# Attention outputs kept by features and divided there by sums that go through memory, in place of two transposes

## The chip, the cores and the metric

The kernel runs as one program on one core of a Trainium2 chip. The time is the device time of one execution in microseconds (us). The kernel before takes 1885.41 us (median of 3 runs, 1884.92 to 1886.67).

The engines have these names in the profile: PE is TensorE (matrix products), PEld its loads of stationary operands, DVE is VectorE, ACT is ScalarE, POOL is GpSimd, SP is SyncE, which here only issues transfers.

## The reference

One encoder layer on x of 1024 tokens by 1024 features, in float32:

```python
h = rms_norm(x, ffn1_norm_g);  x = x + 0.5 * swiglu_ffn(h, ffn1...)
h = rms_norm(x, mix_norm_g);   proj = h @ w_in            # 1024 x 3584
aq, ak, av, hq, hf, hi, hg = jnp.split(proj, 7 x 512)
# A: 8 heads x 64, queries of a 64-token chunk see their own chunk and the 8 before
scores = q_chunk @ k_band.T * 64**-0.5 + bias;  p = softmax(scores);  attn_out = p @ v_band
# B: 4 heads x 128, gated linear recurrence, then a norm and a gate -> hgrn_out
x = x + concat([attn_out, hgrn_out], -1) @ w_out          # 1024x1024 @ 1024x1024
h = rms_norm(x, ffn2_norm_g);  x = x + 0.5 * swiglu_ffn(h, ffn2...)
```

The change touches only what lies between `p @ v_band` and the product with `w_out`.

## The kernel before

The program is written out by hand, engine by engine, with semaphores between them; each engine works its list off in order. A float32 product is made of three faster ones: each operand is split into a high part (`...hi`, written by ACT) and the remainder (`...lo`, written by DVE), and PE multiplies hi by hi, hi by lo and lo by hi (lines 710 to 712). So the left operand of the output projection has to be there as `hThi` and `hTlo`: eight tiles `k` of 128 features, each 128 partitions (features) by 1024 tokens. Tiles 0 to 3 are attention's features (a pair of heads each), 4 to 7 the recurrence's.

Attention goes over four pairs of heads. A pair has 12 units of at most 128x640 scores (two per step, one for each head), so there are 48 units `v` in 24 steps `w`; pair p has the steps 6p to 6p+5. In step w PE issues, in this order: the scores of units 2w and 2w+1 (line 1031); the transposes of the exponentials of unit 2w-2 (`turn`, 1044); the products with v of the two units before (`values(w-2)`, 1064); the transposes of unit 2w-1. Between them `halves` puts transposes of the next pair's q and k (1089), and those of attention's outputs (`turn_out`, 1099). DVE does for each unit `maxima` (bias added, row minimum of the negative, 2123), for two units of three the copy of the transposed exponentials out of PSUM (2134; ACT does the third, 1532), and in steps 1 to 4 of a pair the sums of squares and the normalisation of the next pair's q and k (2087, 2094). ACT makes the exponentials, with their row sums in `psumr` (1549). Scores of step w+1 are written into the banks that `maxima` has read, so PE waits for `unit_max` there.

`values` gives outputs with the features on the partitions and the tokens along the row, not yet divided by the sums of the exponentials. Those sums lie the other way: a token on each partition. So the kernel before does this: ACT copies the output to `outT` (1524); PE turns four 128x128 tiles into bank 7 (`turn_out`, eight times four in all); DVE inverts the sums and multiplies while it copies into `cat` (tokens on the partitions; `head_output`, 2105 and 2109). For the projection, PE turns all of `cat` back, eight transposes per tile of 128 tokens (`turn_cat`, 766, for the first two, `turn_tile`, 751, for the other six), ACT copies the 128x1024 result from PSUM into `hThi` (1222), DVE subtracts into `hTlo` (1654). The recurrence's outputs come into `cat` by a transfer and need this one transpose in any case.

The output projection has 16 rows `d` (8 tiles of tokens times two halves of the output), each of 24 products 128x512. Between the first rows PE issues the transposes of the tile two rows ahead, and after row 0 the last `turn_out`. SP's list around here: q, k, bias and v of the pairs 2 and 3, then the stores of x for the second feed-forward.

Of the kernel before, what the change touches and what calls it, by code (L numbers as in the profile page):

```python
# [24 lines left out]
P = 128  # L25
T = 1024
# [147 lines left out]


OUT_STEPS = NU // 2
# [4 lines left out]


def out_step(p, g):
    return OUT_STEPS * (p + 1) + (0 if g == 0 else 1 if p == PAIRS - 1 else 2)

# [11 lines left out]
def turn_bank(R, t):  # L197

    if R == R_FFN1:
        return (2, 6)[t % 2]  # L200
    if R == R_FFN2:
        return (2, 0, 2, 0, 2, 0, 2, 6)[t]
    if R == R_MIX:
        return (4, 6, 4, 6, 0, 2, 0, 2)[t]
    return 2 * (t % 2)
# [19 lines left out]
def build(nc, x, ffn1_norm_g, ffn1_w_gate, ffn1_w_up, ffn1_w_down, mix_norm_g, w_in, attn_q_norm_g,  # L225
# [3 lines left out]
    with ExitStack() as ctx:  # L229
# [7 lines left out]
        wd_d = nc.dram_tensor("wd_scratch", [4, NPAIR, P, HALF], F32, kind="Internal").ap()  # L237
        x_d = nc.dram_tensor("x_scratch", [T, D], F32, kind="Internal").ap()
# [54 lines left out]
        with ExitStack() as c:  # L293
# [11 lines left out]
            rcp = keep("rcp", [P, 2, 2, TT], where=c)  # L305
            outT = keep("outT", [P, 2, T], where=c)
# [15 lines left out]
        with ExitStack() as c:  # L322
            cat = keep("cat", [P, TT, D], where=c, side="right")
# [107 lines left out]
        lb_diff = sem("lb_diff")  # L431
        lb_sig = sem("lb_sig")
        lb_ready = sem("lb_ready")
# [47 lines left out]
        out_turned = sem("out_turned")  # L481
        rcp_ready = sem("rcp_ready")
        head_out = sem("head_out")
# [22 lines left out]
        def _(sp):  # L506
# [161 lines left out]

            out_pieces(0)
# [36 lines left out]
        def _(pe):  # L706
# [19 lines left out]
            def turn_tile(R, t):  # L726

                r = TT * R + t
                if R == R_CAT:
                    src = cat[:, CAT_ORDER[t], :]  # L730
                    pe.wait_ge(hT_ready, r - 1)
                else:
                    pe.wait_ge(y_ready, TT * norm_no(R) + t + 1)
                    src = y_slot(R, t)
# [20 lines left out]
            def turn_cat(t, h):  # L755


                if h and t == 0:
                    pe.wait_ge(cat_loaded, 16)
                    pe.wait_ge(unit_max, NV)  # L760
                elif h == 0 and t == 0:
                    pe.wait_ge(head_out, 2 * PAIRS - 1)
                c0 = turn_bank(R_CAT, t) * HALF + h * HALF
                for k in range(4):
                    at = h * HALF + k * P
                    mm = pe.transpose(ps[:, c0 + k * P:c0 + (k + 1) * P], cat[:, CAT_ORDER[t], at:at + P], ident[:, :])
                if h == 0:
                    mm.then_inc(turned, 1)
# [300 lines left out]
            def wait_half_bank(what, p, n):  # L1069

                if what == "qk":
                    if n:
                        pe.wait_ge(qkT_ready, 4 * p + n)
                    elif p > 1:
                        pe.wait_ge(head_out, 2 * (p - 2) + 2)
                elif n == 0:
                    if p < PAIRS - 1:
                        pe.wait_ge(qkT_ready, 4 * p + 8)
                    else:
                        pe.wait_ge(head_out, 2 * (p - 1) + 2)  # L1080
                else:
                    pe.wait_ge(head_out, 2 * p + 1)

            def turn_half(p, n):

                pe.wait_ge(qk_normed, 2 * p + n // 2 + 1)
                wait_half_bank("qk", p, n)
# [5 lines left out]
            def turn_out(p, g):  # L1093
                pe.wait_ge(outT_ready, NU * p + (NU - 4 if g == 0 else NU))
                wait_half_bank("out", p, g)
                for t in range(4):
                    c0 = (4 * (1 - g) + t) * P
                    b = 7 * HALF
                    mm = pe.transpose(ps[:, b + t * P:b + (t + 1) * P],
                                      outT[:, p % 2, c0:c0 + P], ident[:, :])  # L1100
                mm.then_inc(out_turned, 1)

            def halves(w, place):
                p, step = w // OUT_STEPS, w % OUT_STEPS
                if place == 0:
                    for g in range(2):
                        for q in range(PAIRS - 1 if g else PAIRS):
                            if out_step(q, g) == w:
                                turn_out(q, g)
# [10 lines left out]
            for w in range(STEPS + 2):  # L1120
# [6 lines left out]
                if w == STEPS:  # L1127
                    turn_cat(0, 1)
                    turn_cat(1, 1)
# [3 lines left out]
                if w == STEPS + 1:  # L1133
                    turn_cat(0, 0)
# [5 lines left out]
            turn_cat(1, 0)  # L1140


            for h in range(2):
                for t in range(TT):
# [3 lines left out]
                    if h == 0 and t == 2:  # L1148
                        pe.wait_ge(head_out, 2 * PAIRS)
# [21 lines left out]
                    if d == 0:  # L1171
                        turn_out(PAIRS - 1, 1)
                    if h == 0 and t + 2 < TT:
                        turn_tile(R_CAT, t + 2)
# [10 lines left out]
        def _(act):  # L1185
# [25 lines left out]
            def hT_hi(R, t):  # L1211
# [3 lines left out]
                if R == R_CAT:  # L1215
                    if t == 0:
                        act.wait_ge(unit_out, NV)
                    t = CAT_ORDER[t]
                elif R == R_MIX:
                    t = MIX_ORDER[t]  # L1220
                src = ps[:, c0:c0 + D].rearrange("p (k c) -> p k c", k=KT)
                act.activation(hThi[:, :, t * P:(t + 1) * P], src, ACT.Copy).then_inc(hT_hi_ready, 1)

# [275 lines left out]
            act.wait_ge(lb_diff, 1)  # L1499
# [926 lines left out]
```

## Time and profile before

| | |
|---|---|
| runs | 1884.92, 1885.41, 1886.67 us |
| profiled execution | 1885.16 us, of which the span from the first to the last instruction is 1883.6 us |
| PE busy | 1869.4 us, 9171 products and transposes |
| DVE, ACT, POOL busy | 1125.0, 675.3, 406.7 us |
| granted TensorE clock | 1.00 over the whole span |
| attention | about 1030 to 1145 us of the span |
| output projection with transposes of `cat` | 1145 to about 1190 us |

Busy time of PE counts each matmul from its start to its modelled end, and these overlap: what one costs is read from the distance between two starts, not from its own duration. "Idle before" in brackets is the time for which the engine stood still ahead of an instruction, and behind it who released it.

### The profile page before, as it was taken

How to read it: one execution, taken by the hardware profiler on the slowest of the kernel's cores; microseconds unless marked ns; L12 is line 12 of the kernel's file. 1: busy time of each engine (PE TensorE's matmuls, PEld its weight loads, DVE VectorE, ACT ScalarE, POOL GpSimd, SP SyncE). 2: the span in 40 equal slices, each digit the busy share in tenths (PEclk: the TensorE clock that was granted, in tenths of full speed). 3: DMA queues.
4: the chain of work that ended last, by engine and by line, in shares of the span. 5: the costliest groups of instructions: out<-in, count | busy, mean ns of one | idle time of the engine just before them, and what ended most of it. 6: DMA issues, size and time to landing. Idle time of an engine off the chain costs nothing. (4 is left out here: it accounts for less than half of the span.)

```text
span 1883.6 us, 24459 instructions
## 1 busy us (share of the span) xinstructions
PE 1869.4 (99%) x9171; PEld 1546.3 (82%) x9171; DVE 1125.0 (60%) x1591; ACT 675.3 (36%) x1029; POOL 406.7 (22%) x319
## 2 busy tenths in 40 slices
PE   9999999999999999999999999999999999999999
PEld 8888888888888888888888678888888888888887
DVE  6966665665546641156667874477666656655464
ACT  7422323333333533211223663353223233333332
POOL 2043422241103110002222310000434222411030
PEclk9999999999999999999999999999999999999999
DMA  5355444436866433434433510133554444368653
GB/s 182 112 196 190 146 162 168 153 138 244 318 195 197 131 122 124 138 101 140 134 132 106 162 60 1 68 112 112 196 190 146 163 167 153 138 244 306 219 192 140
DMA packets 221341, 296.52 MB, mean 157 GB/s; under 512 B 15377, under 2 KB 117913, under 8 KB 221234
## 3 DMA queue, kind: packets, MB, share of 16 engines
q1 hardware_dynamic: 206752, 262.19, 41.0%
q0 software_dynamic: 6272, 18.14, 3.0%
q10 hardware_dynamic: 8210, 14.75, 2.0%
q8 instruction: 68, 1.11, 0.2%
q14 instruction: 39, 0.32, 0.1%
HBM read 206.13 MB, written 92.56 MB: 159 GB/s over the span
## 5 line engine op out<-in xcount | busy, mean ns | idle before, releaser
L710 PE MATMUL ps<-hThi,whi 128*128 128x512 f32 x888 | 346.6, 390 | 0.2 <-DVE hid L1751 0.2
L712 PE MATMUL ps<-hThi,wlo 128*128 128x512 f32 x888 | 345.5, 389 | 0.0
L711 PE MATMUL ps<-hTlo,whi 128*128 128x512 f32 x888 | 345.5, 389 | 0.0
L710 PE MATMUL ps<-whi 128*128 128x512 f32 x616 | 240.0, 390 | 0.0
L712 PE MATMUL ps<-whi,wlo 128*128 128x512 f32 x616 | 239.7, 389 | 0.0
L711 PE MATMUL ps<-wlo,whi 128*128 128x512 f32 x616 | 239.6, 389 | 0.0
L710 PEld LDWEIGHTS ps<-hThi,whi 128*128 128x128 f32 x888 | 166.7, 188 | 34.9 <-issue 0.9
L712 PEld LDWEIGHTS ps<-hThi,wlo 128*128 128x128 f32 x888 | 166.7, 188 | 34.7
L711 PEld LDWEIGHTS ps<-hTlo,whi 128*128 128x128 f32 x888 | 166.7, 188 | 34.3
L710 PE MATMUL ps<-hXhi,whi 128*128 128x512 f32 x480 | 186.9, 389 | 0.8 <-issue 0.8
L712 PE MATMUL ps<-hXhi,wlo 128*128 128x512 f32 x480 | 186.8, 389 | 0.0
L711 PE MATMUL ps<-hXlo,whi 128*128 128x512 f32 x480 | 186.7, 389 | 0.0
L1723 DVE TENSOR_TENSOR wlo<-raw,whi 128x512 fp32r<-128x512 f32 x176 | 127.3, 727 | 98.1 <-ACT whi L1280 98.1
L710 PE MATMUL ps<-whi,hThi 128*128 128x512 f32 x440 | 176.5, 401 | 0.0
L712 PE MATMUL ps<-whi,hTlo 128*128 128x512 f32 x440 | 171.7, 390 | 0.0
L711 PE MATMUL ps<-wlo,hThi 128*128 128x512 f32 x440 | 171.6, 390 | 0.0
L1835 DVE TENSOR_TENSOR wlo<-raw,whi 128x1024 fp32r<-128x1024 f32 x80 | 107.5, 1343 | 80.5 <-ACT whi L1332 80.3
L1280 ACT ACTIVATE whi<-raw 128x512 fp32r<-128x512 f32 x176 | 109.7, 627 | 120.6 <-PE ps L712 120.6
L1835 DVE TENSOR_TENSOR wlo<-rawx,whi 128x1024 fp32r<-128x1024 f32 x74 | 95.2, 1286 | 87.2 <-ACT whi L1332 87.2
L710 PEld LDWEIGHTS ps<-whi 128*128 128x128 f32 x616 | 115.6, 188 | 24.1
L712 PEld LDWEIGHTS ps<-whi,wlo 128*128 128x128 f32 x616 | 115.6, 188 | 23.9
L711 PEld LDWEIGHTS ps<-wlo,whi 128*128 128x128 f32 x616 | 115.6, 188 | 23.8
(220 smaller groups left out, 2828.7 us busy)
## 6 DMA issues: line engine op xcount, KB each, us to landing
hid_scratch<-hid SPq DMA_DIRECT2D x132, 256.0 KB, 3.3
raw<-ffn_w_gate SPq DMA_DIRECT2D x44, 512.0 KB, 3.8
raw<-ffn_w_up SPq DMA_DIRECT2D x44, 512.0 KB, 4.9
wdb<-ffn_w_down SPq DMA_DIRECT2D x44, 512.0 KB, 4.1
wd_scratch<-wdb SPq DMA_DIRECT2D x88, 256.0 KB, 4.3
raw<-hid_scratch SPq DMA_DIRECT2D x80, 256.0 KB, 2.8
rawx<-hid_scratch SPq DMA_DIRECT2D x74, 256.0 KB, 2.8
raw<-w_in SPq DMA_DIRECT2D x28, 512.0 KB, 5.4
```

The lines of the kernel that those rows point to most:

```text
L710: pe.matmul(dst, ahi, bhi, start=first, stop=False, skip_group_check=onto)
L711: pe.matmul(dst, ahi, blo, start=False, stop=False, skip_group_check=onto)
L712: return pe.matmul(dst, alo, bhi, start=False, stop=last, skip_group_check=onto)
L1280: act.activation(weight(whi, w, F), raw_weight(w), ACT.Copy).then_inc(w_hi_ready, 1)
L1723: dve.tensor_tensor(weight(wlo, w, F), raw_weight(w), weight(whi, w, F).bitcast(F32), ALU.subtract).then_inc(w_ready, 1)
L1835: dve.tensor_tensor(wlo[:, s, :], raw_piece(n), whi[:, s, :].bitcast(F32), ALU.subtract)\
```

## The change

- ACT copies attention's outputs to `catT`, which holds all four pairs by features (128 x 4 x 1024). `turn_out` and the multiplication out of bank 7 are gone, and with them the waits of q's and k's transposes for that bank.
- DVE inverts the sums of a pair at once (`invert_sums`, at unit 2 of the next pair; for the last pair in two halves, at units 45 and 48). SP stores the inverses to memory (`store_rcp`), tokens in order, and loads them back as rows, each repeated on the 64 partitions of its head (`load_rcp`, to `rowr`). DVE multiplies `catT` by `rowr` in place, 128x512 at a time (`norm_out`, at units 9 and 11 of the next pair; for the last pair behind the loop and behind `add(1)`).
- Only the recurrence's half (`cath`) is turned for the projection, four transposes per tile of tokens into one bank of four, four tiles ahead (`turn_cat`). ACT and DVE write `hThi` and `hTlo` in two instructions each, one from PSUM and one from `catT` (`cat_hi`, `cat_lo`).
- Three semaphores of the lower bound `lb` become one.

```diff
-def out_step(p, g):
-    return OUT_STEPS * (p + 1) + (0 if g == 0 else 1 if p == PAIRS - 1 else 2)
+def cat_bank(t):
+    return t % 4
...
+        rcp_d = nc.dram_tensor("rcp_scratch", [PAIRS, TT, 2, P], F32, kind="Internal").ap()
...
-            rcp = keep("rcp", [P, 2, 2, TT], where=c)
-            outT = keep("outT", [P, 2, T], where=c)
+            rcp = keep("rcp", [P, 2, TT, 2], where=c)
+            rowr = keep("rowr", [P, 2, T], where=c)
...
-            cat = keep("cat", [P, TT, D], where=c, side="right")
+            catT = keep("catT", [P, PAIRS, T], where=c, side="right")
+            cath = keep("cath", [P, TT, HALF], where=c, side="right")
...
+            def store_rcp(p, g=None):
+                tiles = slice(0, TT) if g is None else slice(4 * (1 - g), 4 * (1 - g) + 4)
+                sp.wait_ge(rcp_ready, p + 1 + (g or 0))
+                sp.dma_start(rcp_d[p, tiles].rearrange("t h p -> p (t h)"),
+                             rcp[:, p % 2, tiles, :].rearrange("p t h -> p (t h)"),
+                             allow_slow_non_contiguous=True).then_inc(rcp_stored, 16)
+            def load_rcp(p, g=None):
+                tiles = slice(0, TT) if g is None else slice(4 * (1 - g), 4 * (1 - g) + 4)
+                sp.wait_ge(rcp_stored, 16 * (p + 1 + (g or 0)))
+                if p >= 2:
+                    sp.wait_ge(out_normed, 2 * (p - 2) + 2)
+                for hd in range(2):
+                    row = rcp_d[p, tiles, hd:hd + 1, :].rearrange("t h p -> h t p")
+                    sp.dma_start(rowr[hd * DH:(hd + 1) * DH, p % 2, tiles.start * P:tiles.stop * P]
+                                 .rearrange("r (t p) -> r t p", p=P),
+                                 row.to_broadcast([DH, tiles.stop - tiles.start, P])).then_inc(row_loaded, 16)
...
                 load_qk(p)
+                store_rcp(p - 2)
                 sp.wait_ge(unit_out, NU * (p - 1))
                 load_bias(p)
                 load_v(p)
+                load_rcp(p - 2)
+            store_rcp(PAIRS - 2)
+            load_rcp(PAIRS - 2)
+            for g in range(2):
+                store_rcp(PAIRS - 1, g)
+                load_rcp(PAIRS - 1, g)
...
-            def turn_out(p, g):
-                pe.wait_ge(outT_ready, NU * p + (NU - 4 if g == 0 else NU))
-                wait_half_bank("out", p, g)
-                for t in range(4):
...
-                if p >= 2 and 2 * w % NU == 0:
-                    act.wait_ge(out_turned, 2 * (p - 2) + 2)
...
-                    last = act.activation(outT[:, p % 2, t * P:(t + 1) * P], ps[:, b:b + P], ACT.Copy)
+                    last = act.activation(catT[:, p, t * P:(t + 1) * P], ps[:, b:b + P], ACT.Copy)
...
+            def cat_hi(t):
+                act.wait_ge(turned, TT * R_CAT + t + 1)
+                if t == 0:
+                    act.wait_ge(unit_out, NV)
+                at = slice(CAT_ORDER[t] * P, (CAT_ORDER[t] + 1) * P)
+                act.activation(hThi[:, 4:KT, at], bank(cat_bank(t)).rearrange("p (k c) -> p k c", k=4), ACT.Copy)
+                act.wait_ge(out_normed, 2 * PAIRS - (1 if t < 4 else 0))
+                act.activation(hThi[:, 0:4, at], catT[:, :, at], ACT.Copy).then_inc(hT_hi_ready, 1)
...
-            def head_output(p, g):
...
+            def norm_out(p, g):
+                cols = slice(HALF * (1 - g), HALF * (1 - g) + HALF)
+                dve.wait_ge(row_loaded, 32 * (p + 1 + (g if p == PAIRS - 1 else 0)))
+                dve.wait_ge(outT_ready, NU * p + (NU - 4 if p == PAIRS - 1 and g == 0 else NU))
+                dve.tensor_tensor(catT[:, p, cols], catT[:, p, cols], rowr[:, p % 2, cols], ALU.mult)\
+                   .then_inc(out_normed, 1)
...
+                if v == NV - 3:
+                    invert_sums(PAIRS - 1, 0)
+                if v >= NU and v < NV:
+                    p = v // NU - 1
+                    if v % NU == 2:
+                        invert_sums(p)
+                    if v % NU in (9, 11):
+                        norm_out(p, (v % NU - 9) // 2)
+                if v == NV:
+                    invert_sums(PAIRS - 1, 1)
+            norm_out(PAIRS - 1, 0)
+            cat_lo(0)
+            cat_lo(1)
```

How the instructions stand now. First DVE at step 6 (units 12 and 13, the first of pair 1): `ISA S,nmax` is one unit's `maxima`, `COPY PT` the copy of transposed exponentials. Before:

```order
L2134 COPY PT<-ps 128x640 [waits unit_out,unit_turned]
L2105 RECIPROCAL rcp<-psumr 128x2x4 [waits unit_exp,ro_stored]
L2109 TENSOR_TENSOR cat<-ps,rcp 128x4x128 [waits out_turned,rcp_ready]
L2123 ISA S,nmax<-ps,bias 128x640 [waits unit_exp,unit_scores]
L2123 ISA nmax 128x1
L2123 ISA S,nmax<-ps,bias 128x640 [waits unit_exp,unit_scores]
```

and now:

```order
L2137 COPY PT<-ps 128x640 [waits unit_out,unit_turned]
L2126 ISA S,nmax<-ps,bias 128x640 [waits unit_exp,unit_scores]
L2126 ISA nmax 128x1
L2126 ISA S,nmax<-ps,bias 128x640 [waits unit_exp,unit_scores]
L2126 ISA nmax 128x1
L2137 COPY PT<-ps 128x640 [waits unit_out,unit_turned]
L2105 RECIPROCAL rcp<-psumr 128x2x8 [waits unit_exp]
L2126 ISA S,nmax<-ps,bias 128x640 [waits unit_exp,unit_scores]
```

The reciprocal and the multiplication no longer stand between the two maxima of step 6; a reciprocal of twice the width stands between those of step 7. Next PE from the last `turn_out` of the attention loop to the projection's first product. Before:

```order
L1099 MATMUL ps<-ident,outT 128x128 [waits head_out,outT_ready]
L1099 MATMUL ps<-ident,outT 128x128 x3
L1064 MATMUL ps<-PT,v_in 64x128 [waits outT_ready,PT_by_vector,PT_by_scalar]
L1064 MATMUL ps<-PT,v_in 64x128 x9
L1044 MATMUL ps<-ident,Pr 128x128 [waits PT_by_vector,unit_exp]
L1044 MATMUL ps<-ident,Pr 128x128 x4
L766 MATMUL ps<-ident,cat 128x128 [waits head_out]
L766 MATMUL ps<-ident,cat 128x128 x3
L1064 MATMUL ps<-PT,v_in 64x128 [waits outT_ready,PT_by_scalar,PT_by_vector]
L1064 MATMUL ps<-PT,v_in 64x128 x9
L766 MATMUL ps<-ident,cat 128x128 x4
L720 MATMUL ps<-whi,hThi 128x512 [waits split_lo,hT_hi_ready]
```

and now:

```order
L1084 MATMUL ps<-PT,v_in 64x128 [waits outT_ready,PT_by_vector,PT_by_scalar]
L1084 MATMUL ps<-PT,v_in 64x128 x9
L1064 MATMUL ps<-ident,Pr 128x128 [waits PT_by_vector,unit_exp]
L1064 MATMUL ps<-ident,Pr 128x128 x4
L786 MATMUL ps<-ident,cath 128x128 x4
L1084 MATMUL ps<-PT,v_in 64x128 [waits outT_ready,PT_by_scalar,PT_by_vector]
L1084 MATMUL ps<-PT,v_in 64x128 x9
L786 MATMUL ps<-ident,cath 128x128 x4
L747 MATMUL ps<-whi,hThi 128x512 [waits split_lo,hT_hi_ready]
```

The four transposes of `outT` are gone there, and the transposes of the recurrence's half need nothing of DVE. Last DVE from the copy of unit 45 to the projection's first subtractions, now:

```order
L2137 COPY PT<-ps 128x640 [waits unit_out,unit_turned]
L2113 TENSOR_TENSOR catT<-catT,rowr 128x512 [waits outT_ready,row_loaded]
L2137 COPY PT<-ps 128x640 [waits unit_out,unit_turned]
L2105 RECIPROCAL rcp<-psumr 128x2x4 [waits unit_exp]
L2113 TENSOR_TENSOR catT<-catT,rowr 128x512 [waits outT_ready,row_loaded]
L1651 TENSOR_TENSOR hTlo<-ps,hThi 128x4x128 [waits hT_hi_ready]
L1653 TENSOR_TENSOR hTlo<-catT,hThi 128x4x128
L1651 TENSOR_TENSOR hTlo<-ps,hThi 128x4x128 [waits hT_hi_ready]
L1653 TENSOR_TENSOR hTlo<-catT,hThi 128x4x128
```

Before, the projection's first subtraction followed upon the last copy, one reciprocal and one multiplication; now a multiplication that waits for a transfer (`row_loaded`) stands ahead of it.

## Rows read from the trace of the kernel before

**Rows 1.** The page, busy time of each engine.

```profile
PE 1869.4 (99%) x9171; PEld 1546.3 (82%) x9171; DVE 1125.0 (60%) x1591; ACT 675.3 (36%) x1029; POOL 406.7 (22%) x319
```

**Rows 2.** PE's waits over the span: total us, times, longest.

```profile
PE ps L1031 <- DVE nmax L2123: 3.0, 6, 0.8
```

**Rows 3.** Transposes of cat and outT: ns min/median/max, first and last start.

```profile
L751 PE MATMUL ps<-ident,cat x48: 270/272/273, 1151.1 to 1183.6; 128*128 128x128 f32 x48
...
L766 PE MATMUL ps<-ident,cat x16: 272/273/328, 1137.4 to 1144.2; 128*128 128x128 f32 x16
...
L1099 PE MATMUL ps<-ident,outT x32: 270/272/273, 1058.3 to 1151.0; 128*128 128x128 f32 x32
```

**Rows 4.** PE's timeline, steps 6 to 9: start, us, what, idle before.

```profile
1056.45 1.35 PE L1031 MATMUL ps<-kT,qT 64*128 64x512 f32 x8
...
1061.02 1.35 PE L1031 MATMUL ps<-kT,qT 64*128 64x512 f32 x8 [0.15 <-DVE nmax L2123]
...
1064.94 1.35 PE L1031 MATMUL ps<-kT,qT 64*128 64x512 f32 x8
...
1069.37 1.35 PE L1031 MATMUL ps<-kT,qT 64*128 64x512 f32 x8
```

**Rows 5.** DVE's timeline, steps 6 to 12 and step 22.

```profile
1059.31 0.19 DVE L2105 RECIPROCAL rcp<-psumr 128x8 f32<-128x8 f32 x1
1059.54 0.69 DVE L2109 TENSOR_TENSOR cat<-ps,rcp 128x512 f32<-128x512 f32 x1
...
1060.89 0.08 DVE L2123 DVE_READ_ACCUMULATOR2_ANT nmax<- 128x1 f32 x1
...
1063.89 0.81 DVE L2123 CUSTOM_DVE_ANT_0 S<-ps,bias 128x640 f32<-128x640 f32 x1
...
1080.00 0.82 DVE L2134 COPY PT<-ps 128x640 f32<-128x640 f32 x1
...
1081.72 0.56 DVE L2123 CUSTOM_DVE_ANT_0 S<-ps,bias 128x384 f32<-128x384 f32 x1 [0.90 <-PE ps L1031]
...
1084.80 0.82 DVE L2134 COPY PT<-ps 128x640 f32<-128x640 f32 x1 [1.34 <-PE ps L1044]
...
1086.07 0.82 DVE L2123 CUSTOM_DVE_ANT_0 S<-ps,bias 128x640 f32<-128x640 f32 x1 [0.45 <-PE ps L1031]
...
1133.72 0.82 DVE L2134 COPY PT<-ps 128x640 f32<-128x640 f32 x1 [0.18 <-PE ps L1044]
```

**Rows 6.** PE's timeline around row 1 of the projection.

```profile
1150.67 0.60 PE L1099 MATMUL ps<-ident,outT 128*128 128x128 f32 x4
1151.11 1.04 PE L751 MATMUL ps<-ident,cat 128*128 128x128 f32 x8
...
1157.48 1.03 PE L751 MATMUL ps<-ident,cat 128*128 128x128 f32 x8
```

**Rows 7.** Timeline at the projection's start, ACT and PE.

```profile
1143.98 1.02 ACT L1222 ACTIVATE hThi<-ps 128x1024 fp32r<-128x1024 f32 x1 [1.51 <-PE ps L1064]
...
1145.06 0.50 PE L720 MATMUL ps<-whi,hThi 128*128 128x512 f32 x1 [0.59 <-ACT hThi L1222]
```

**Rows 8.** ACT's copies of half that width, from the first feed-forward.

```profile
L1227 ACT ACTIVATE hThi<-ps x8: 578/593/623, 11.1 to 23.8; 128x512 fp32r<-128x512 f32 x8
```

**Rows 9.** DMA issues: KB each, median us from issue to landing.

```profile
raw<-ffn_w_gate SPq DMA_DIRECT2D x44, 512.0 KB, 3.8
...
raw<-hid_scratch SPq DMA_DIRECT2D x80, 256.0 KB, 2.8
...
tok_scratch<-y ACTq DMA_DIRECT2D x40, 256.0 KB, 2.0
...
v_in<-tok_scratch SPq DMA_DIRECT2D x4, 512.0 KB, 5.4
...
bias_scratch<-tot POOLq DMA_DIRECT2D x2, 128.0 KB, 5.5
...
lbs<-hgrn_lower_bounds POOLq DMA_DIRECT2D x1, 4.0 KB, 4.8
```

More of the change, by code:

```diff
@@ L728, in turn_tile @@
                 r = TT * R + t
[L729 to L734, printed above, removed]
+                pe.wait_ge(y_ready, TT * norm_no(R) + t + 1)
+                src = y_slot(R, t)
                 if R == R_MIX:
@@ L1091, in turn_half @@
                 mm.then_inc(qk_turned, 1)
-            def turn_out(p, g):
-                pe.wait_ge(outT_ready, NU * p + (NU - 4 if g == 0 else NU))
-                wait_half_bank("out", p, g)
-                for t in range(4):
[L1097 to L1101, printed above, removed]
-            def halves(w, place):
[L1104 to L1109, printed above, removed]
+            def halves(w, place):
+                p, step = w // (NU // 2), w % (NU // 2)
                 if p + 1 < PAIRS:
@@ L1139, in _ @@
                 halves(w, 1)
-            turn_cat(1, 0)
+            turn_cat(3)
             for h in range(2):
@@ L1170, in _ @@
                     mm.then_inc(row_done, 1)
[L1171 to L1174, printed above, removed]
+                    if h == 0 and t + 4 < TT:
+                        turn_cat(t + 4)
                     if h == 1 and t >= 1:
@@ L1498, in _ @@
             group(0, 0, ACT.Silu, True)
-            act.wait_ge(lb_diff, 1)
-            act.activation(lb[:, 0, :], lb[:, 2, :], ACT.Sigmoid).then_inc(lb_sig, 1)
-            act.wait_ge(lb_ready, 1)
+            act.wait_ge(lb_step, 1)
+            act.activation(lb[:, 0, :], lb[:, 2, :], ACT.Sigmoid).then_inc(lb_step, 1)
+            act.wait_ge(lb_step, 3)
             group(1, 0, ACT.Sigmoid, True)
@@ L1557, in _ @@
                 if v == NV + 2:
-                    hT_hi(R_CAT, 0)
+                    cat_hi(0)
                 if v >= 4 and v % 2 == 0:
@@ L1564, in _ @@
             for t in range(1, TT):
-                hT_hi(R_CAT, t)
+                cat_hi(t)
             for q in range(4):
@@ L1655, in hT_lo, with cat_lo @@
                                   hThi[:, k0:KT, t * P:(t + 1) * P].bitcast(F32), ALU.subtract)\
+                   .then_inc(hT_ready, 1)
+            def cat_lo(t):
+                dve.wait_ge(hT_hi_ready, TT * R_CAT + t + 1)
+                at = slice(CAT_ORDER[t] * P, (CAT_ORDER[t] + 1) * P)
+                dve.tensor_tensor(hTlo[:, 4:KT, at], bank(cat_bank(t)).rearrange("p (k c) -> p k c", k=4),
+                                  hThi[:, 4:KT, at].bitcast(F32), ALU.subtract)
+                dve.tensor_tensor(hTlo[:, 0:4, at], catT[:, :, at], hThi[:, 0:4, at].bitcast(F32), ALU.subtract)\
                    .then_inc(hT_ready, 1)
@@ L2098, in _, with invert_sums @@
                           lambda: norm_qk(0, 1)])
-            def head_output(p, g):
-                tiles = slice(4 * (1 - g), 4 * (1 - g) + 4)
-                dve.wait_ge(unit_exp, NU * p + (NU if g else NU - 4))
-                dve.reciprocal(rcp[:, p % 2, :, tiles], psumr[:, p % 2, :, tiles]).then_inc(rcp_ready, 1)
-                dve.wait_ge(rcp_ready, 2 * p + g + 1)
-                dve.wait_ge(out_turned, 2 * p + g + 1)
-                r = rcp[:, p % 2, :, tiles].rearrange("p h t -> p t h").unsqueeze(3).to_broadcast([P, 4, 2, DH])
-                dve.tensor_tensor(cat[:, tiles, p * P:(p + 1) * P].rearrange("p t (h d) -> p t h d", d=DH),
-                                  bank(7).rearrange("p (t h d) -> p t h d", t=4, d=DH), r, ALU.mult)\
-                   .then_inc(head_out, 1)
+            def invert_sums(p, g=None):
+                tiles = slice(0, TT) if g is None else slice(4 * (1 - g), 4 * (1 - g) + 4)
+                dve.wait_ge(unit_exp, NU * p + (NU - 4 if g == 0 else NU))
+                if p >= 2 and not g:
+                    dve.wait_ge(rcp_stored, 16 * (p - 1))
+                dve.reciprocal(rcp[:, p % 2, tiles, :].rearrange("p t h -> p h t"), psumr[:, p % 2, :, tiles])\
+                   .then_inc(rcp_ready, 1)
+            def norm_out(p, g):
[4 more added lines that the diff above has]
+                   .then_inc(out_normed, 1)
             dve.wait_ge(proj_done, PROJ_OUTS)
@@ L2169, in _ @@
                 add(t, CAT_ORDER[t], 0)
+                if t == 1:
+                    norm_out(PAIRS - 1, 1)
                 if t + 2 < TT:
-                    hT_lo(R_CAT, t + 2)
+                    cat_lo(t + 2)
             for t in range(TT):
```

80 lines of the change are left out of this document (24 added, 56 removed).

## The prediction

> **What bounds the kernel now.** I read the page's busy times first: PE is busy for 1869.4 us of 1883.6 [rows 1], so what PE does is paid almost everywhere. PE's waits come next, to see where the few idle microseconds lie: 3.0 us in six places before scores, for DVE's row maxima, the longest 0.8 [rows 2], and 0.59 us before the first product of the output projection, for ACT's copy to `hThi` [rows 7]. Both lie inside the stretch that the change touches, so there PE's work alone doesn't decide: each place needs a look at whether DVE or ACT ends close behind PE. For that I read the timelines of PE and DVE over attention's steps, then the start of the projection. The reader is to see three things in them: the pitch of the steps, how late DVE's last maximum is against PE's next scores, and which instruction comes just before the first product of the projection.
>
> **What PE loses.** 96 transposes concern `outT` and `cat`: 48, 16 and 32 [rows 3]. Of them 32 (`outT`) go and 32 of the 64 of `cat` go. Their own 272 ns is not their price, since they overlap: four cost 1151.11 - 1150.67 = 0.44 us when they stand in a row with others [rows 6], 0.11 each. So:
>
> - Projection, 32 transposes of `cat`: 32 x 0.11 = 3.5 us. A row with eight of them lasts 1157.48 - 1151.11 = 6.37 us [rows 6]; ACT's copy takes 1.02 of that [rows 7], and two of half the width 1.2 [rows 8], so the split copies are hidden behind PE there, and DVE's, which are some 0.2 longer as well.
> - The last `turn_out`, behind row 0: 0.44 us.
> - The `turn_out` of the last pair in step 24: 0.44 to 0.53, I take 0.5; the steps' own rows say the same as follows.
>
> **Attention's steps.** Step 6 lasts from 1056.45 to 1061.02, 4.57 us; step 7, without `turn_out`, 3.92; step 8, with one, 4.43 [rows 4]. So step 6 has 0.65 too much and step 8 0.51 too much. In step 6 four transposes (0.44) don't explain all of it: PE's next scores waited 0.15 us for DVE [rows 4], whose last maximum ended at 1060.97 [rows 5], because the multiplication into `cat` (0.69 us, at 1059.54) stood between the two maxima. The change takes both away, the transposes from PE and the multiplication from DVE's place between the maxima. Without them DVE's last maximum would end some 0.9 earlier, and PE's 3.92 decides. The pattern comes three times (pairs 1 to 3): 3 x (0.65 + 0.51) = 3.5 us. The third pair gives nearly the same, so I don't correct for it.
>
> What comes in instead:
> - The reciprocal of a pair, now in steps 7, 13, 19 between the maxima. Bounds: nothing, or its whole 0.19 (for half the width) [rows 5]. In step 7 DVE's last maximum starts at 1063.89 and ends about 0.8 later, at 1064.7, PE's scores start at 1064.94 [rows 4, 5]: the cover is about 0.2 before a semaphore's way. I take 0.1 each, 0.3 in all.
> - `norm_out` at unit 9 of a pair, behind the copy that starts at 1080.00 and ends at 1080.82: DVE is then idle for 0.90 until 1081.72 [rows 5], and a 128x512 multiplication takes 0.69 from PSUM (its row), from SBUF I take 0.73. Hidden. At unit 11 it stands behind the copy that starts at 1084.80; the next maximum started at 1086.07 after 0.45 idle, so it is 0.2 to 0.3 late. That step is a former step 6 or 12 with its 0.2 of slack: I take 0.1 in all, between 0 and 0.6.
> - ACT's copies to `catT` are those to `outT`, and waits for bank 7 only go.
>
> **The start of the projection.** The first product waits for ACT's copy, which starts at 1143.98 and takes 1.02 [rows 7]. Now it is two copies of half the width, 0.59 each [rows 8], which overlap by some 0.05 to 0.1: 0.1 to 0.2 more, I take 0.15. The second of them waits for `norm_out` of the last pair, and that for the row of inverse sums: a store and two loads behind the reciprocal at unit 45. This is the only new wait on PE's path with no great cover, and it holds all that is behind it: `cat_hi` on ACT with the last `keep_out`, `cat_lo` on DVE, and the projection's first product on PE.
>
> Its cover: the reciprocal follows the copy of 1133.72, so it ends near 1134.7 [rows 5]. The second copy of ACT would start at 1143.98 + 0.5 less the 0.5 us of the gone `turn_out`, about 1144.0, and `norm_out` takes 0.73 and some 0.1 to be seen. So store plus loads have about 8.5 us. For pair 2 the time from the reciprocal (unit 38, near 1120.7) to its use (unit 45, 1134.5, less 0.4 of step 20) is about 13.5 us; for pairs 0 and 1, from 1064.1 to 1080.7 less 0.5, about 16 us.
>
> Its price: no row shows a store of 4-byte pieces. The store of the last pair's half has 1024 of them, of a whole pair 2048. From below: a store of 128 rows, 2.0 us. From above: 512 pieces of 256 bytes to memory took 5.5 (`bias_scratch<-tot`); less 2.0 that is 6.8 ns a piece, so 9.0 for 1024 and 16 for 2048. Nearest in kind is the load of 1024 values of 4 bytes, `lbs`, 4.8 us on POOL's queue; I take it, and 2.0 + 2 x 2.8 = 7.6 for 2048. The loads have pieces of 512 bytes: two of 128 KB together like one of 256 KB, 2.8, with the second issue 3.0; of a whole pair 1024 pieces and 512 KB, 3.8 as `raw<-ffn_w_gate`, at worst 5.4 as `v_in` [rows 9]. So the last half needs 4.8 + 3.0 + 0.2 for semaphores = 8.0 of 8.5, pair 2 needs 7.6 + 3.8 + 0.2 = 11.6 of 13.5, the first two pairs 11.6 of 16, where bias and v loads stand between on SP's list, but are issued at once. All hidden, with 0.5 us to spare at the tightest place. I take 0 for it, with -0 to +4 as its range there.
>
> The Trainium skill, page "DMA: Bandwidth & Descriptors", speaks against this store in two places: its overview gives 512 bytes as the least piece for full rate, with read-modify-write below, and its list of patterns (the row on a strided last dimension) says that such a transfer becomes one descriptor per element. The row of `lbs` bears the second out at most weakly (4 KB took 4.8 us, 256 KB took 2.0), and no row shows the first at 4 bytes. By the page's measured table (10.5 ns for each packet on one of 16 engines, 2 us fixed) the store would take an estimated 2.7 us and not come near its cover. What a slow store would do is the first rival.
>
> **Sum.** -3.5 (cat transposes) -0.44 (last turn_out) -0.5 (turn_out of step 24) -3.5 (steps 6, 8 and their like) +0.3 (reciprocals) +0.1 (norm_out) +0.15 (two copies) = -7.4 us. From the profiled execution's 1885.16: 1877.8. The median of the runs is 0.25 above the profiled one, so 1878.1 us.
>
> **The rivals.**
> - *The row comes late (slower at the far end).* Let e be what 1024 pieces cost beyond 2.0 us (I took 2.8). The last half starts to hold PE at e = 8.5 - 2.0 - 3.2 = 3.3, pair 2 at (13.5 - 6.0)/2 = 3.75, pairs 0 and 1 at (16 - 6.0)/2 = 5. DVE's wait for a row stops maxima and copies, and PE within one step. Mild case, e = 5: about 2.5 at pair 2 and 1 or 2 at the end, total 1878.1 + 4 = 1882. Bad case, e = 7 (the corner stores' rate): 6.5 + 2 x 4, with the end covered by the stop at pair 2, which lets the last store go out while DVE stands: +14.5, total 1892.6. Slower than before by 0.2% needs e above 6.4. For it: one row at that rate per piece. Against: those pieces were 64 times as large, and on POOL's queue, whose 4-byte load took less for twice the pieces [rows 9].
> - *DVE sets the pace of the steps.* If in the steps with 3.92 us DVE's round (scores, maximum, copy, maximum) is the real bound, and the gains of steps 6 and 8 were only DVE's, nothing is lost; but if the new reciprocal and norm_out cost their full time, 3 x 0.2 + 3 x 0.7, the gain there is 0.8 instead of 3.1: 1880.4. For it: the ends in rows 4 and 5 are within 0.2 us of each other. Against: norm_out stands where rows show 0.90 and 0.45 of idle time.
> - *The stretch gives nothing in attention:* another wait (ACT's exponentials) keeps the steps at 4.5; then only 4.2 are left: 1881.2. Against: step 7 has the same ACT work and runs at 3.92.
>
> **How the numbers follow.** Forecast 1878.1, chance 0.70; row late, mild 0.12 (1880 to 1884), bad 0.04; DVE's pace 0.08; nothing in attention 0.04; the remaining 0.02 for a gain above 8.2, if PE's wait at the projection shrinks as well. A measurement of this kernel can tell about 0.2%, 3.8 us, from no change: faster is below 1881.6. The forecast, DVE's pace, half of the mild case and most of the fourth are faster: 0.86, which I lower to 0.83 for what I don't see; same 0.12; slower 0.05. The range 1877.0 to 1882.5 holds the forecast with its unknown costs (1877.2 to 1879), both pace cases and half of the mild one.
>
> **What the profile of the changed kernel would show.** PE with 9107 instructions (64 fewer); steps 6, 8, 12, 14, 18, 20 at 3.9 to 4.0 us between scores, as step 7; rows of the projection at 5.9 us, and 5.5 for the last ones, in place of 6.3; DVE's idle time before `norm_out` on a DMA near zero for pairs 0 to 2; `rcp_scratch<-rcp` landing in 3 to 8 us; the first product's wait for ACT still about 0.6 to 0.8 us. The forecast is wrong if PE waits more than 1 us there, if DVE waits for `rowr`, or if scores wait for maxima in steps 7 and 12 by more than 0.3.

## The result and the profile after

The changed kernel takes 1896.44 us (median of 4 runs, 1894.51 to 1898.25) against 1885.18 before (median of 4 runs): ratio 1.0058, interval 1.0046 to 1.0070. It is slower by 0.6%, where 1878.1 us, faster by 0.4%, was forecast. Its profiled execution took 1894.51 us, with a span of 1892.3.

The page of the changed kernel, busy time of each engine, answers to [rows 1]:

```profile
PE 1864.7 (99%) x9107; PEld 1541.7 (81%) x9107; DVE 1123.0 (59%) x1596; ACT 676.2 (36%) x1037; POOL 407.9 (22%) x319
```

PE has its 64 instructions fewer. Its waits, total us, times, longest, answer to [rows 2]:

```profile
PE ps L747 <- ACT hThi L1216: 9.5, 1, 9.5
PE ps L1051 <- DVE nmax L2126: 2.5, 3, 0.8
PE ps L1064 <- ACT PT L1524: 2.5, 2, 1.3
...
PE ps L786 <- DVE nmax L2126: 1.4, 1, 1.4
```

Scores wait for maxima three times, no longer six. But the projection's first product waits 9.5 us where it was 0.59 [rows 7], and there are two new kinds of wait. The timeline of all engines around that product shows the chain behind it:

```profile
1146.13 0.66 PE L786 MATMUL ps<-ident,cath 128*128 128x128 f32 x4
1146.30 0.60 ACT L1214 ACTIVATE hThi<-ps 128x512 fp32r<-128x512 f32 x1 [1.51 <-PE ps L1084]
...
1154.88 0.69 DVE L2113 TENSOR_TENSOR catT<-catT,rowr 128x512 f32<-128x512 f32 x1 [11.80 <-DMA rowr<-rcp_scratch]
1155.61 0.63 ACT L1216 ACTIVATE hThi<-catT 128x512 fp32r<-128x512 f32 x1 [8.72 <-DVE catT L2113]
...
1156.29 0.79 PE L747 MATMUL ps<-whi,hThi 128*128 128x512 f32 x1 [9.50 <-ACT hThi L1216]
```

PE waits for ACT's second copy, that for `norm_out` on DVE, and that, for 11.80 us, for the row. SP's timeline shows why the row is late: it issues the loads only when the store before them has landed. Its columns are start, time to issue, queue and line.

```profile
1121.24 0.37 SPq L673 DMA_DIRECT2D rcp_scratch<-rcp  x1
1132.66 1.26 SPq L685 DMA_DIRECT2D rowr<-rcp_scratch  x2
1136.22 0.36 SPq L673 DMA_DIRECT2D rcp_scratch<-rcp  x1
1147.30 1.24 SPq L685 DMA_DIRECT2D rowr<-rcp_scratch  x2
1148.58 0.60 SPq L673 DMA_DIRECT2D rcp_scratch<-rcp  x1
1158.32 1.24 SPq L685 DMA_DIRECT2D rowr<-rcp_scratch  x2
```

The store of pair 2 (2048 values) took 11.42 us from its issue to that of the loads, that of the last pair's first half (1024 values) 11.08, the second half 9.74. The view of the transfers over the first of these stores, 1121.0 to 1132.6 in 40 slices, shows where its time isn't:

```profile
DMA  0000677720000000000000000000000000000000
...
DMA packets 2064, 0.01 MB, mean 1 GB/s; under 512 B 2064, under 2 KB 2064, under 8 KB 2064
```

The line DMA is the busy share of the DMA engines in tenths, slice by slice. All packets are through in some 1.5 us (slices 5 to 9 of 0.29 us), and then nothing is seen on any of the DMA engines for 9.0 us, until the semaphore comes. So the time does not go into the packets on the engines but lies behind them; what it goes into there, the profile does not show.

The steps of attention answer to [rows 4], PE's timeline, steps 6 to 9:

```profile
1056.19 1.35 PE L1051 MATMUL ps<-kT,qT 64*128 64x512 f32 x8
...
1060.11 1.35 PE L1051 MATMUL ps<-kT,qT 64*128 64x512 f32 x8
...
1064.02 1.35 PE L1051 MATMUL ps<-kT,qT 64*128 64x512 f32 x8
...
1067.94 1.35 PE L1051 MATMUL ps<-kT,qT 64*128 64x512 f32 x8
```

Steps 6 and 8 last 3.92 us, as step 7: the forecast of 0.65 and 0.51 came true to the hundredth. And in the projection the rows have a pitch of 5.94 in place of the 6.33 to 6.37 us of before, PE's transposes of `cath` ahead of rows 2 and 3:

```profile
1169.18 0.60 PE L786 MATMUL ps<-ident,cath 128*128 128x128 f32 x4
...
1175.12 0.60 PE L786 MATMUL ps<-ident,cath 128*128 128x128 f32 x4
```

So the gains are there, and what was lost lies in a few places. The table of stretches (length, busy times, then granted clock, DMA share, GB/s) shows one more thing at two of them:

```profile
1106.00:1108.00 2.00, 2.00 (x14) 1.67 (x16) 2.00 (x3) 1.55 (x5) 0.00 (x0) 0.50 1.18 301
...
1146.00:1150.00 4.00, 0.79 (x8) 0.42 (x4) 0.00 (x0) 0.60 (x1) 0.00 (x0) 0.87 0.25 63
1150.00:1152.00 2.00, 0.00 (x0) 0.00 (x0) 0.00 (x0) 0.00 (x0) 0.00 (x0) 0.50 0.29 16
...
1156.00:1158.00 2.00, 1.71 (x4) 1.42 (x5) 1.68 (x3) 2.00 (x7) 0.00 (x0) 0.50 0.00 0
```

The granted clock, 1.00 everywhere in the kernel before, was 0.50 (1.2 GHz) in the later part of PE's stop and for its first products afterwards, and it was 0.50 behind the stop in step 16 too.

### The profile page after: what moved, and what is told of

Read it like the earlier page. It is cut to its first block and busy times, and to the rows that moved or that the text cites. A ratio compares the mean times of both kernels' runs of the same rounds, so it can differ in the third digit from the quotient of the medians.

```text
span 1892.3 us, 24356 instructions
## 1 busy us (share of the span) xinstructions
PE 1864.7 (99%) x9107; PEld 1541.7 (81%) x9107; DVE 1123.0 (59%) x1596; ACT 676.2 (36%) x1037; POOL 407.9 (22%) x319
```

## The experiments

All are variants of the changed kernel. Store times below are read as above, from SP's issue of the store to its issue of the loads that wait for it: "pair" is the store of pair 2 (2048 values), "half" the next one (1024 values). Theory A: the whole loss hangs on the store. Its rival B: the rearrangement costs something itself. Each variant was run in one set with the kernel before, and its ratio is to that: in the set of e1 to e4 this took 1885.77 us, in that of e5 to e8 1884.99, in that of e9 to e11 1886.17.

**No rows (e1_norows).**

```diff
             def store_rcp(p, g=None):
+                return
...
             def load_rcp(p, g=None):
+                return
...
-                dve.wait_ge(row_loaded, 32 * (p + 1 + (g if p == PAIRS - 1 else 0)))
+                dve.wait_ge(row_loaded, 1)
...
+            pool.memset(rowr[:, :, :], 0.01).then_inc(row_loaded, 1)
```

> Leaves out the way through memory: no store and no loads, the rows are a constant 0.01, written once by GpSimd (so the division is by the wrong numbers); all else as in the changed kernel. Theory A (the whole loss is the store, whose semaphore comes 10 to 12.5 us after its issue): 1878.1 us as forecast, plus or minus 1, steps 6 to 20 at 3.92 us, PE's wait at the projection 0.6 to 0.8 us, ACT's unexplained stops of 1 to 2 us in steps 10, 16 and 22 gone. Theory B (the rearrangement itself, split copies and moved multiplications, costs something too): above 1880, with DVE or ACT releasing scores late in steps 7, 12, 13.

Measured: 1878.22 us (5 runs, 1878.03 to 1878.91), ratio 0.9962 (0.9949 to 0.9975). Its first product of the projection, from the timeline:

```profile
1141.50 0.50 PE L749 MATMUL ps<-whi,hThi 128*128 128x512 f32 x1 [0.68 <-ACT hThi L1218]
```

The wait is 0.68 us, and scores wait for maxima three times as in the changed kernel. The forecast sum, 1878.1, is the time of everything but the store and the loads. B expected more than 1880 and scores released late in other steps; neither is seen.

**Stored partition by partition (e2_contig).** The same bytes in 128 pieces of 64 bytes.

```diff
-                sp.dma_start(rcp_d[p, tiles].rearrange("t h p -> p (t h)"),
+                sp.dma_start(rcp_d[p, tiles].rearrange("t h p -> (t h p)").rearrange("(p q) -> p q", p=P),
```

> The inverse sums are stored partition by partition: 128 pieces of 64 bytes (32 for the halves) in place of 2048 (1024) of 4; the same bytes, the same loads, which now find them in another order (so the division is by the wrong numbers). Theory A1 (pieces of 4 bytes that many DMA engines write into the same 64-byte line wait for one another): the store lands in 2 to 3 us, time 1878 to 1880. Theory A2 (each write to memory below 512 bytes has a long completion of its own): still near 10 us, time near 1893 to 1896. Theory A3 (a price for each piece): 128 pieces, so 2 to 3 us as in A1.

Measured: 1878.32 us (1878.10 to 1878.49), ratio 0.9961 (0.9946 to 0.9976). SP's timeline:

```profile
1117.84 0.34 SPq L673 DMA_DIRECT2D rcp_scratch<-rcp  x1
1119.27 1.26 SPq L685 DMA_DIRECT2D rowr<-rcp_scratch  x2
1131.43 0.34 SPq L673 DMA_DIRECT2D rcp_scratch<-rcp  x1
1132.87 1.24 SPq L685 DMA_DIRECT2D rowr<-rcp_scratch  x2
```

1.43 and 1.44 us. With this one line changed, the whole loss is gone, with all loads and waits in place. A2, a long completion for each write below 512 bytes, has fallen: pieces of 64 or 32 bytes are not slow. In the halves two of the 32-byte pieces share a 64-byte line, and that costs nothing that shows (1.44 against 1.43).

**As many pieces, 64 bytes apart (e3_apart64).**

```diff
+        rcp_w = nc.dram_tensor("rcp_wide", [PAIRS, TT, 2, P, 16], F32, kind="Internal").ap()
...
-                sp.dma_start(rcp_d[p, tiles].rearrange("t h p -> p (t h)"),
+                sp.dma_start(rcp_w[p, tiles, :, :, 0].rearrange("t h p -> p (t h)"),
```

> As many pieces of 4 bytes as in the changed kernel (2048, 1024), but each 64 bytes from the next, so that no two share a 64-byte line; the loads read another place of memory, filled with the identity once at the start (the division is by the wrong numbers). A1 (shared lines): the store lands in 3 to 5 us, time 1878 to 1882. A3 (a price for each piece): 10 to 12 us as before, time 1893 to 1897. If pieces share something wider, a row of 512 bytes: in between.

Measured: 1878.28 us (3 runs, 1878.09 to 1878.50), ratio 0.9961 (0.9946 to 0.9976). SP's timeline:

```profile
1118.30 0.36 SPq L674 DMA_DIRECT2D rcp_wide<-rcp  x1
1122.61 1.26 SPq L686 DMA_DIRECT2D rowr<-rcp_scratch  x2
1131.90 0.37 SPq L674 DMA_DIRECT2D rcp_wide<-rcp  x1
1134.54 1.24 SPq L686 DMA_DIRECT2D rowr<-rcp_scratch  x2
```

4.31 and 2.64 us with the same number of 4-byte pieces. A3, a price for each piece alone, has fallen; where the pieces lie against one another decides, as A1 says. The transfers over the store of pair 2, 1118.0 to 1123.0 in 40 slices of 0.125 us:

```profile
DMA  0000000000777777777600000000000000000000
```

The packets again take some 1.3 us; the semaphore then comes 2.1 us behind them (1122.61), where it was 9.0. So the layout changes the time behind the packets.

**The repair (e4_turned).** PE turns the inverse sums, so that SP stores whole rows.

```diff
+            rcpT = keep("rcpT", [2 * TT, 2, P], where=c)
...
-                sp.dma_start(rcp_d[p, tiles].rearrange("t h p -> p (t h)"),
-                             rcp[:, p % 2, tiles, :].rearrange("p t h -> p (t h)"),
-                             allow_slow_non_contiguous=True).then_inc(rcp_stored, 16)
+                sp.dma_start(rcp_d[p, tiles].rearrange("t h p -> (t h) p"),
+                             rcpT[0:2 * (tiles.stop - tiles.start), i % 2, :]).then_inc(rcp_stored, 16)
...
+                pe.transpose(ps[0:n, 7 * HALF:7 * HALF + P], rcp[:, p % 2, tiles, :].rearrange("p t h -> p (t h)"),
+                             ident[:, :]).then_inc(rcp_ready, 1)
...
+                act.activation(rcpT[0:n, i % 2, :], ps[0:n, 7 * HALF:7 * HALF + P], ACT.Copy).then_inc(rcp_ready, 1)
```

> PE turns the 128x16 (128x8) inverse sums into bank 7 (one transpose for each store, five in all), ACT copies them to a tile of 16 partitions, and SP stores 16 (8) pieces of 512 bytes; loads, multiplications and results as in the changed kernel. Theory A: the store lands in 2 to 2.5 us, the rows are there before norm_out for pairs 0 to 2; at the projection's start turn, copy, store and loads need about 1 + 0.3 + 2.2 + 3.5 us of 8.5, so PE waits 0.6 to 1.5 us there; 1878.5 to 1880 us, faster than before by 5 to 7 us. Theory B: above 1882.

Measured: 1878.57 us (5 runs, 1878.37 to 1879.65), ratio 0.9964 (0.9951 to 0.9978): 0.36% faster than before, with nothing of the computation left out. From its timeline, the store and the loads of the last pair's first half, the multiplication that waits for them, and the first product:

```profile
1133.50 0.34 SPq L675 DMA_DIRECT2D rcp_scratch<-rcpT  x1
...
1134.73 1.24 SPq L686 DMA_DIRECT2D rowr<-rcp_scratch  x2
...
1138.57 0.69 DVE L2143 TENSOR_TENSOR catT<-catT,rowr 128x512 f32<-128x512 f32 x1 [1.22 <-DMA rowr<-rcp_scratch]
...
1141.74 0.50 PE L748 MATMUL ps<-whi,hThi 128*128 128x512 f32 x1 [0.62 <-ACT hThi L1232]
```

The row is there 2.5 us before ACT's second copy, and 1.8 before it if the multiplication is taken off. PE's price for the turn shows in the steps that hold one: 4.02 us between scores in steps 8 and 14, where e1_norows has 3.91. Of all that was run it is the best kernel that does the whole computation.

**How the pieces lie: four, eight, none to a row, and one partition's own lines.** All with `rcp_w` as in e3_apart64, its last dimension 4, 2 or 128, and for the two "own" kernels

```diff
+        rcp_w = nc.dram_tensor("rcp_wide", [PAIRS, 2, P, 2 * TT, 2], F32, kind="Internal").ap()   # 16 in e9_own64
...
+                sp.dma_start(rcp_w[p, g or 0, :, 0:2 * (tiles.stop - tiles.start), 0],
```

> The pieces of 4 bytes stand 16 bytes apart, so four share a 64-byte line, where it is 16 in the changed kernel and one in the kernel with 64 bytes between them; the loads read another place, as there. Theory L1 (a piece that is written into a line with other pieces in flight waits for each of them; 16 in a line cost about 8 us beyond the 2.8 to 4 us of the kernel with 64 bytes between, so 0.5 us a piece): four cost about 2 us, the halves land in 4.5 to 5 us and the pairs' store in 5.5 to 7. Rival W (what is shared is the row of 512 bytes, 128 pieces in the changed kernel and 32 here, 8 with 64 bytes between): nearly the same, about 4.5 to 5.5 us. Rival Z (any sharing of a line brings the whole stop): 10 to 11 us. Time 1878 to 1880 with L1 and W, above 1890 with Z.

> As many pieces of 4 bytes, 8 bytes apart, and the 16 values of one partition next to one another: a 64-byte line holds eight pieces, all of one partition, which one DMA engine writes one after the other. Theory L1 (each piece waits for the others in its line, whoever writes them): eight cost about 4 us, the halves land in 6.5 to 7.5 us. Theory L2 (only pieces of different DMA engines wait for one another, one engine's are taken in order): as with 64 bytes between, 2.8 us for the halves and 4 to 5.5 for the pairs. Time 1878 to 1880 with L2, 1879 to 1884 with L1.

> Pieces 8 bytes apart across partitions, eight to a 64-byte line and 64 to a row of 512 bytes (loads from another place). So far: sixteen to a line 9.7 to 12.7 us, four 3.5 to 3.9 (halves) and 7.0 to 7.5 (pairs), one 2.6 to 3.0 and 4.3 to 5.8. If the price grows with the number in a line (about 0.5 us each): halves 5 to 7 us, pairs 7.5 to 9.5, time 1878 to 1881. If it jumps only when a whole line or row is filled: as with four, 3.5 to 4 and 7 to 7.5.

> The values of one partition next to one another again, but 64 bytes apart, so that no two share a 64-byte line, while eight share a row of 512 bytes and are written one after the other by one DMA engine (loads from another place). If the 64-byte line is what is shared: as with 64 bytes between partitions, halves 2.6 to 3.5 us, pairs 4.3 to 5.8. If it is the row of 512 bytes: as with 8 bytes between them, 5.3 to 5.7 and 11 to 13.

> Pieces of 4 bytes, 512 bytes apart: no two share a row of 512 bytes either (loads from another place). If the row still costs something with 64 bytes between pieces: halves below 2.5 us, pairs below 4. If only the 64-byte line matters: as with 64 bytes, 2.6 to 3.0 and 4.3 to 5.8.

**Fewer pieces in full lines (e7_fewer).**

```diff
-                sp.dma_start(rcp_d[p, tiles].rearrange("t h p -> p (t h)"),
-                             rcp[:, p % 2, tiles, :].rearrange("p t h -> p (t h)"),
+                sp.dma_start(rcp_d[p, tiles.start:tiles.start + 1].rearrange("t h p -> p (t h)"),
+                             rcp[:, p % 2, tiles.start:tiles.start + 1, :].rearrange("p t h -> p (t h)"),
```

> The changed kernel's layout, but of each store only the first tile's sums go out: 256 pieces in place of 2048 or 1024, 16 in each line as before; 16 lines in place of 128 or 64 (the loads read places filled once at the start). L1 and L2 (the price is set by how many share one line, since different lines go side by side): still 9 to 11 us for every store, time 1892 to 1897. Rival (the price is for each piece that shares): an eighth to a quarter of it, 3 to 4 us, time 1878 to 1880.

Store times in us, each from SP's timeline in one profile, and the kernel's time (a single run except in the first, second and last row):

| 4-byte pieces | to a 64-byte line | pair, 2048 | half, 1024 | kernel, us |
|---|---|---|---|---|
| changed kernel, 4 bytes from partition to partition | 16 | 11.42 | 11.08 | 1896.44 |
| e3_apart64 | 1 | 4.31 | 2.64 | 1878.28 |
| e10_apart8 | 8 | 8.41 | 4.78 | 1879.19 |
| e5_apart16 | 4 | 7.01 | 3.90 | 1877.79 |
| e11_apart512 | 1, alone in 512 bytes | 3.96 | 2.55 | 1877.60 |
| e6_own, one partition's 8 bytes apart | 8 | 11.18 | 5.33 | 1885.60 |
| e9_own64, one partition's 64 bytes apart | 1 | 5.99 | 4.23 | 1878.69 |
| e7_fewer, 256 pieces in both | 16 | 8.12 | 8.05 | 1885.34 |
| e2_contig (64 and 32 bytes a piece) | 1 (pair), 2 (half) | 1.43 | 1.44 | 1878.32 |

What follows. With 1024 pieces and the neighbours in memory from neighbouring partitions, the store gets slower step by step as they lie closer: 2.6, 3.9, 4.8, 11.1 us for a half with 1, 4, 8 and 16 to a 64-byte line. In full lines the number of pieces matters less: 256 took 8.1 where 1024 took 11.1. With up to eight in a line it does matter: the pairs cost 1.4 to 2.1 times the halves in six of the layouts.

The width of the stretch that the pieces share is not shown. Where more share a 64-byte line, more share a row of 512 bytes too (8, 32, 64 and 128 for the four halves above), so rival W of e5_apart16, the row, fits the order as well as the line does. Only its lower end is settled: eight to a row add little (4.31 against 3.96, 2.64 against 2.55). Nor is sharing all of it. With one piece to a line and eight to a row, e9_own64 took 5.99 and 4.23, e3_apart64 4.31 and 2.64; they differ in the order, a partition's own values side by side or those of its neighbours, and why that costs 1.6 us is open.

The rules on record for the size did not hold. L1, 0.5 us for each piece in the line, gave 6.5 to 7.5 us for the half of e6_own (5.33) and 9 to 11 us for the stores of e7_fewer, with 1892 to 1897 for the kernel (8.1 and 1885.34; its rival, 3 to 4 us, missed too). L2, that pieces of one partition don't wait for one another, gave 2.8 us for the half of e6_own and 4 to 5.5 for its pair; they took 5.33 and 11.18, against 4.23 and 5.99 for the same order 64 bytes apart. The halves of e5_apart16 and e10_apart8 (3.90 and 4.78) came out below the 4.5 and 5 that were expected at least, and e9_own64 fell between the two ranges given for its half. Store times also differ by up to 1.3 us within one kernel: the last pair's second half, beside the loads of the first, took 9.74 in the changed kernel (11.08 the first), 5.75 in e10_apart8 (4.78) and 9.05 in e7_fewer (8.05). So it is shown that the loss comes from 4-byte pieces of different partitions lying close together in memory; the exact rule, the line of 64 bytes included, is not.

**PE kept busy while it waits (e8_warm).**

```diff
             turn_cat(3)
+            idle_turns(80)
```

> The changed kernel with 80 transposes of the identity (0.11 us each, 8.8 us) on PE while it waits ahead of the projection's first product, so that it isn't idle there. The wait for the row is unchanged (the first product starts within 0.5 us of where it did), but the granted clock stays at 1.0 and the first six products take 0.23 us each from start to start in place of 0.43: 1.2 us less than the changed kernel in the profile. Rival: the clock costs nothing that counts, same time. Against the kernel before it stays slower by 7 to 12 us.

Measured: 1900.16 us (2 runs, 1899.92 and 1900.41), slower than the changed kernel and not faster, and the first product starts 7.0 us later than there. In its profile DVE waited 6.15 us for the row of pair 2 (1.83 in the changed kernel); the loads of that pair, beside the next store, took 8.97 us to land. PE stood 5.68 us there, and its clock fell at that place (0.72 from 1140 to 1150). From the timeline, what stands before the first product:

```profile
1154.66 8.90 PE L1108 MATMUL ps<-ident 128*128 128x128 f32 x80
1154.83 0.63 ACT L1217 ACTIVATE hThi<-catT 128x512 fp32r<-128x512 f32 x1
...
1163.32 0.49 PE L747 MATMUL ps<-whi,hThi 128*128 128x512 f32 x1
```

The long stop had moved to pair 2, ahead of the idle transposes, and when these began the last row was there: ACT's second copy ended at 1155.46, and the transposes held PE until 1163.32. They cost some 7.9 us themselves, more than the 3.7 by which this kernel is slower. So the run tests nothing of the clock: there was no stop left in that place to fill, and the clock was back at 1.00 before the idle transposes began. What the clock costs is read from the changed kernel, where the products behind the stop start 0.43 us apart, and from e1_norows, where they start 0.23 apart. From the first product to the ninth it is 3.29 us against 1.95 (1156.29 to 1159.58, 1141.50 to 1143.45), so 1.3 us. Whether keeping PE busy would win them back was not tested.

## Why the prediction was wrong

**The sum of the parts was right.** Transposes of `cat`, `turn_out`, steps 6 and 8, the reciprocals, the two copies: -7.4 us were forecast, and without the store the kernel takes 1878.22 to 1878.32, where the sum said 1878.1. The overlap price of a transpose (0.11 and not its 272 ns) and the reading that both PE's transposes and DVE's multiplication had to go from steps 6 and 8 carried this. Scores waited for maxima nowhere new, so the rivals on DVE's pace and on attention's gain are out. In the changed kernel the gains are the same, and the store takes them back.

**The step that failed is the store's price.** I took 4.8 us for 1024 values, the load of `lbs`, as nearest in kind, with 2.0 and 9.0 as ends. It took 11.1, beyond my upper end. Three things in that step were wrong. A load with 4-byte pieces stood for a store with 4-byte pieces, though the load's pieces are not written close together in memory. The upper end came from stores whose pieces of 256 bytes are not close together in that sense either. And the price was made proportional to the number of pieces, which let the half, the one store on PE's path, look safe: in this layout half the pieces saved 0.3 us of 11.4. The pairs' stores (12.6, 12.7 and 11.4 us where I took 7.6) stayed within my ends (16) and held DVE for 4.6 us in all three (16.4 less 11.8), as against 14.5 in the bad case; but the half was given up to 9.0 and PE's cover was 8.5. The loads were off too: they landed 6.9 us after issue at the end where I had 3.0 for both, with the next store on the queue 1.28 us behind the first of them. This term alone would have made the row late: in e10_apart8 the half's store took 4.78 us, just what I had taken, but from the issue of the loads to the multiplication 5.1 us passed, and PE waited 1.97 us at the projection in place of 0.68. From the reciprocal's end to the multiplication the changed kernel needed 18.7 us (11.1 for the store, 7.6 for the loads) where 8.0 were forecast and about 8.5 were covered; the difference to the cover, 10.2, is close to the 10.0 lost there.

That the row would come late was on my list of rivals, with 0.04 for the bad case. But its total, 1892.6, was put together from stops at the pairs, with the end covered by them; measured, most of the loss is one stop at the projection. That the total comes near the measured 1896.4 is luck. The range ended at 1882.5 because the cost's own upper end was given hardly any weight. Of the two warnings from the Trainium skill (page "DMA: Bandwidth & Descriptors") that I set beside it, the trace agrees with the one in the list of patterns, one descriptor per element: 2064 packets for 2048 values. The one in the overview, 512 bytes as the least piece for full rate with read-modify-write below, is not what decided: pieces of 64 bytes landed in 1.43 us, single ones of 4 bytes in 2.55 (halves), and no run shows the read-modify-write. The page's 10.5 ns a packet and 2 us fixed, by which the half would take an estimated 2.7 us, come near 2.55 and 2.64, measured for neighbouring partitions with one piece to a line; 4.23 was measured for a partition's own, and 11.1 for sixteen to a line.

**Where the 16 us between 1878 and 1894.5 are**, from PE's timelines of the changed kernel and of e1_norows: 10.0 between step 23's scores and the projection's first product (21.14 against 11.10), of which 8.8 are the wait for ACT's copy (9.50 against 0.68) and 1.35 the wait for maxima that DVE's stop at pair 2 brought; 1.4 in row 0, 1.3 of them the half clock (6.95 against 5.58); 1.3, 2.4 and 1.4 in steps 10, 16 and 22 (6.64, 7.78 and 5.30 against 5.38, 5.38 and 3.92). With 0.15 in step 11 and 0.45 less ahead of step 6 the sum is 16.2, the spans differ by 16.0. In step 16 a part is the half clock again: from the 20 products with v to what follows them it is 1.75 us, where e1_norows has 1.25.

The stops in steps 10, 16 and 22 come ahead of DVE's wait for the row and are ACT's. In ACT's timeline of the changed kernel, step 22:

```profile
1131.69 0.70 ACT L1524 ACTIVATE PT<-ps 128x640 f32<-128x640 f32 x1 [2.09 <-remote]
```

ACT stood for 2.09 us with nothing on the core that it waited for, and went on 1.0 us before SP issued the loads (1132.66); in the other two pairs likewise, 1074.85 against 1075.81 and 1103.27 against 1104.44. In e8_warm, with the same stores, the stops are there too, but end 0.1, 1.5 and 1.2 us before the loads. In the kernels with a fast store there is no such stop, and in two with a slow one there is none either: with 11.18 us in e6_own and 8.12 in e7_fewer, steps 10, 16 and 22 lasted 5.38, 5.38 and 3.92. So a late semaphore alone does not bring them; they were seen only with 2048 pieces in full lines. Whether the store causes them, and by what way, is open.

## What to carry to other kernels

A store that puts 4-byte values from neighbouring partitions side by side in memory is not a small transfer: turn the tile on TensorE first (some 0.1 us and a copy of 0.25) and store rows. Where a change puts a transfer through memory on the path, its cover has to be larger than the worst end of its price, and a price for a form of transfer that no row shows isn't bounded by rows of another direction or layout. A short measurement of that one transfer would have settled this case.

## What the runs showed of the hardware

- 1024 values of 4 bytes from 128 partitions to memory: 11.1 us with 16 to a 64-byte line, 2.6 us with one, 1.44 us as pieces of 32 bytes. Of the 11.4 us of a pair's store, the 2048 packets took about 1.5, and for the last 9.0 the DMA engines are seen idle.
- Transfers beside such a store land late. The loads of bias issued right behind the stores of pairs 0 and 1 landed in 14.3 and 14.5 us, those of v in 15.3 and 16.1; in the kernel before it was 4.1, 3.8, 5.1 and 4.9, with e2_contig 4.1, 4.3, 5.2 and 5.8.
- At the end of a stop of PE of 9.5 us the granted clock was 0.50, and stayed there for the first products, 0.43 us apart where it is 0.23 at 1.00. The same level was granted at the end of the stops of 5.45 us in e7_fewer and 5.68 in e8_warm.
- An engine can stand for 1 to 2 us with no semaphore of its own core to wait for: ACT, in three places of the changed kernel and of e8_warm, and only where the stores of 2048 values filled whole lines.
